# Dealing an expert's rows over the DMA engines from four starting points in turn instead of one

## The reference, cut to what matters

```
idx = top_k(where(expert_mask, choice, -inf), 8)       # 8 of 64 experts for each of 512 tokens
w = 2.5 * s[idx] / sum(s[idx])
for each expert e:                                     # w_exp_up[e]: 1024x512, w_exp_down[e]: 256x1024, float32
    y = (silu(gate) * up) @ w_exp_down[e],  (gate, up) = split(u[tokens of e] @ w_exp_up[e])
    acc[tokens of e] += y * w
out = x + acc + shared_expert(u)
```

```
56 54 80 82 64 63 80 56 85 67 67 66 83 64 43 61 57 49 63 58 77 69 57 78 53 61 68 58 51 58 77 68
62 58 79 62 58 62 49 48 86 82 66 53 51 47 47 64 66 52 59 45 64 48 77 56 63 76 73 71 70 66 75 88
```

## Time and profile before

| | us |
|---|---|
| median of 3 runs | 1267.52 |
| lowest, highest | 1266.24, 1271.38 |
| the profiled execution, its own time | 1268.87 |
| its span in the trace | 1267.0 |
| PE busy | 1168.9 (92%) |
| DVE busy | 918.3 (72%) |
| ACT busy | 724.0 (57%) |
| POOL busy | 238.0 (19%) |
| weights and other direct transfers (q1) | 250.88 MB, 56.0% of 16 engines' span |
| gathers and scatters (q0) | 33.87 MB, 11.6% |

### The profile page before, as it was taken

One profiled execution on the slowest core, in us unless ns is written; L12 is line 12 of the kernel. 1 busy time (PEld: TensorE's weight loads), 2 busy tenths in 40 slices (PEclk: granted clock), 3 DMA queues, 4 the chain that ended last, 5 costly groups with the idle time before them and its releaser, 6 DMA issues.

```text
span 1267.0 us, 17831 instructions
## 1 busy us (share of the span) xinstructions
PE 1168.9 (92%) x5911; PEld 883.1 (70%) x5911; DVE 918.3 (72%) x1343; ACT 724.0 (57%) x926; POOL 238.0 (19%) x146
## 2 busy tenths in 40 slices
PE   4999998999999899898999999999999999999993
PEld 3699987766677788565777666667666666666662
DVE  4576477544433693667999999889889888988882
ACT  7443333334333322425778777777777777777772
POOL 1000000000000000001343342333333332333331
PEclk9999998999999999899999999999999999999998
DMA  6312231212121323727999999999999999999992
GB/s 215 125 58 93 83 112 47 75 59 66 33 67 64 120 100 100 286 76 265 345 353 349 359 365 358 352 347 347 345 342 353 351 343 350 341 345 346 345 291 35
DMA packets 133357, 285.29 MB, mean 225 GB/s; under 512 B 11876, under 2 KB 34424, under 8 KB 133316
## 3 DMA queue, kind: packets, MB, share of 16 engines
q1 hardware_dynamic: 118580, 250.88, 56.0%
q0 software_dynamic: 14736, 33.87, 11.6%
HBM read 272.11 MB, written 29.38 MB: 238 GB/s over the span
## 4 chain that ended last, share of the span: by engine, by line
PE 46%; DMA 31%; DVE 9%; ACT 7%; issue 4%; SPq 1%; DVEq 0%; POOL 0%; POOLq 0%; ACTq 0%
PE bank L1370 36%; DMA arena<-in_w_exp_up_dram 16%; DMA arena<-in_w_exp_down_dram 12%; ACT split L521 5%; DVE split L1258 4%; PE bank L1538 2%; PE bank L1565 2%; DMA arena<-u_rows,arena 2%; PE bank L1449 1%; ACT arena L521 1%; PE bank L1682 1%; PE bank L1550 1%; PE bank L1701 1%; DMA arena<-in_x_dram 1%; DVE arena L944 0%
## 5 line engine op out<-in xcount | busy, mean ns | idle before, releaser
L1258 DVE TENSOR_TENSOR split<-arena,split 128x2048 fp32r<-128x2048 f32 x192 | 438.9, 2287 | 70.1 <-ACT split L521 68.8
L521 ACT ACTIVATE split<-arena 128x2048 fp32r<-128x2048 f32 x192 | 366.9, 1917 | 93.5 <-DMA arena<-in_w_exp_up_dram 76.0
L1370 PE MATMUL bank<-split,gatheredT 128*96 128x512 f32 x1536 | 374.2, 399 | 7.2 <-DVE gatheredT L1265 3.0
L1370 PEld LDWEIGHTS bank<-split,gatheredT 128*96 128x96 f32 x1536 | 244.6, 163 | 112.2 <-issue 5.8
L1370 PE MATMUL bank<-split,hidT 128*96 128x512 f32 x768 | 191.9, 398 | 1.5 <-ACT arena L521 1.5
L474 POOL DMA_INDIRECT arena<-u_rows,arena x64 | 128.4, 2007 | 251.7 <-DVE arena L1274 194.1
L1370 PEld LDWEIGHTS bank<-split,hidT 128*96 128x96 f32 x768 | 119.1, 162 | 47.0 <-issue 1.6
L482 POOL DMA_INDIRECT out_dram<-arena x64 | 101.7, 1589 | 257.7 <-ACT arena L521 180.1
L1370 PE MATMUL bank<-hT_high,front_split 128*128 128x512 f32 x448 | 143.9, 403 | 0.8 <-DVE hT_low L852 0.8
L521 ACT ACTIVATE arena<-bank 96x512 f32<-96x512 f32 (+4 forms) x217 | 107.7, 532 | 57.5 <-PE bank L1370 29.2
L1370 PEld LDWEIGHTS bank<-hT_high,front_split 128*128 128x128 f32 x448 | 81.4, 189 | 28.1 <-issue 11.5
(11 more groups left out here) (237 smaller groups left out, 1346.1 us busy)
## 6 DMA issues: line engine op xcount, KB each, us to landing
arena<-in_w_exp_up_dram SPq DMA_DIRECT2D x128, 1024.0 KB
arena<-in_w_exp_down_dram SPq DMA_DIRECT2D x64, 1024.0 KB
arena<-in_w_in_dram SPq DMA_DIRECT2D x14, 1024.0 KB, 5.5
arena<-in_w_in_dram SPq DMA_DIRECT2D x10, 768.0 KB, 4.5
arena<-in_w_branches_dram SPq DMA_DIRECT2D x4, 1024.0 KB, 5.0
arena<-in_w_out_dram SPq DMA_DIRECT2D x4, 1024.0 KB, 4.9
arena<-in_x_dram SPq DMA_DIRECT2D x4, 512.0 KB, 5.4
arena<-in_w_mem_kv_dram SPq DMA_DIRECT2D x2, 1024.0 KB, 5.2
```

Source lines behind the costliest of these rows:

```text
L521: return nc.scalar.activation(o, i, ACT.Copy, **kw)
L1258: v.tensor_tensor(both[:, 1], raw[q % RAW], both[:, 0].bitcast(F32), ALU.subtract).then_inc(low_done, 1)
L1370: ins = mm(bank, left[a], right[b], start=first and q == 0, stop=last and q == 2)
```

## The change

Before, the place in the list alone sets the DMA engine: place 0 is always on engine 0, and an expert with 70 tokens gives five rows to engines 0 to 5 and four to the others. After, there are four row assignments. Expert e uses number e % 4 (`n % TURN`), in which place p lies on engine (p + 4 * (e % 4)) % 16: the dealing begins at engine 0, 4, 8 or 12. The order of the tokens in their list, the number of rows, and what is computed for each token are the same.

The assignment leaves the stack of seven square constants (128 x 896 words become 128 x 768), and the four are a constant of their own, 128 partitions x 4 x 96 words (196,608 bytes), loaded by SP with one more transfer into the place of `out_norm`. DVE waits for three small transfers (48) in place of two (32).

```diff
-    spread = np.where(c < ROWS, c % SHARE * DMA_ENGINES + c // SHARE, c)
-    square = np.stack([r == c, r + c == P - 1, np.broadcast_to(c, (P, P)), r < c, np.ones((P, P)), level,
-                       np.broadcast_to(spread, (P, P))], 1)
+    square = np.stack([r == c, r + c == P - 1, np.broadcast_to(c, (P, P)), r < c, np.ones((P, P)), level], 1)
...
+    row, turn = np.arange(ROWS)[None, :], np.arange(TURN)[:, None]
+    spread = row % SHARE * DMA_ENGINES + (row // SHARE - turn * (DMA_ENGINES // TURN)) % DMA_ENGINES
...
+        "spread": np.ascontiguousarray(np.broadcast_to(spread, (P, TURN, ROWS)), dtype=np.float32),
...
-        square = at(take(7, P), 7, P)
-        ident, flip, counting, before, ones, level, spread = (square[:, n, :] for n in range(7))
+        square = at(take(6, P), 6, P)
+        ident, flip, counting, before, ones, level = (square[:, n, :] for n in range(6))
...
-        out_norm = at(take(BV), BV)
+        out_norm_at = take(BV)
+        out_norm = at(out_norm_at, BV)
+        spread = at(out_norm_at, TURN, ROWS)
...
             sp.dma_start(rs[:, 616:620], const["tokens"]).then_inc(c_in[9], 16)
+            sp.dma_start(spread, const["spread"]).then_inc(c_in[9], 16)
...
-            dve.wait_ge(c_in[9], 32)
+            dve.wait_ge(c_in[9], 48)
...
-                v.tensor_tensor(select[:, n % 2, :, :], bcast(spread[:, None, 0:ROWS], P, NT, ROWS),
+                v.tensor_tensor(select[:, n % 2, :, :], bcast(spread[:, n % TURN, None, :], P, NT, ROWS),
```

## The result

The changed kernel takes 1252.85 us (median of 4 runs, 1252.08 to 1253.92) against 1266.88 before (1265.52 to 1271.38): 14.0 us less, ratio 0.9884, 95% interval 0.9858 to 0.991. The direction was right, the size was not: 14.0 us in place of 8.8. Run again later it took 1252.04 beside 1266.95 (0.9884, 0.9863 to 0.9904), 14.9 us less.

A forecast was written before the change was run, and what follows sets the result against it. The prediction took the busiest DMA engine to bound the expert stage. Dealing gained 8.8 us, all other parts nothing: 1268.87 - 8.8 = 1260.1 us profiled, 1259 us as a median, range 1253.5 to 1266.5.

The forecast's parts named there:

- what bounds: Expert stage: goes at the DMA engines' pace, 10.4 us an expert against PE's 9.7 to 9.9; engine 0 fullest, 283 rows.
- the price of a row: Gathers and scatters on queue q0: 0.267 us a row in one direction, 0.53 us for gather and scatter.
- the sum's single term: Dealing from engine 0, 4, 8, 12: fullest engine 266 rows in place of 283, 8.8 us gained.
- A: Rival: DMA engines share one limit, so even dealing gives nothing; 1267.5 us, give or take 2; chance 0.12.
- The constants: Smaller square constant, 65,536 bytes less before the first weights: 0 to 0.3 us gained, taken as nothing.
- the limit that the prediction cites: Trainium skill page: memory side binds transfers at about 358 GB/s a core; if so, no gain, 1267.5 us.
- B: Rival: compute side, PE at 9.9 us an expert, takes half of the 8.8 us; 1263 us; chance 0.15.
- C: Rival: lag averages out, all DMA engines run at the mean, 14 us gained; 1253.5 us; chance 0.08.
- D: Rival: an engine slow by itself, such as 15, loses its cover; slower, 1275 us at a 23 us handicap; chance 0.03.
- the tail: Sign at the end of the weight stream: DMA share drops at once, without some five slices at 1 or 2 tenths.
- ACT's last waits: Sign at the end of the stream: ACT's waits of 1 to 2 us for the last weight blocks shrink.
- The time before 600 us: Sign for the part before 600 us: the same as before the change within 1 us.

The follow-up runs named there:

- filling up 15 engines beside the busiest: Changed kernel, empty rows of all engines gather row 511, against only engine 0's rows doing so: 1289.29 us against 1282.85.
- added gathers: Changed kernel (1252.04 us) with empty rows gathering row 511: 1282.85 us for engine 0's rows only, 1289.29 for all engines.
- added scatters: Changed kernel with scatters to a scratch table, 1255.20 us; the same with every empty row scattered too, 1286.81 us.
- only engine 0 filled: Changed kernel with only engine 0's empty rows gathering row 511: 1282.85 us, beside 1266.98 for the kernel before.

## Why the prediction came out wrong in size

**Right: what bounds.** The stage is bound by the DMA engines and, for most of the time, by the busiest. One, two and four starts are faster in the order of their fullest totals (sixteen against four is within the noise), the lags between the engines are those of the row totals, and filling up 15 engines beside the busiest costs only 6.4 us. The start at engine 8 shows that the fullest total is not all: the same total took 6 us more.

**Right: the price of a row.** 0.53 us in the forecast, 0.53 to 0.59 by the pairs of kernels with added gathers and with added scatters. With 0.32 and 0.27 the step of 17 gathers and 16 scatters is 9.8 us, with 0.26 and 0.27 it is 8.7.

**Wrong: the sum's single term.** The step that failed is "17 gathers and 16 scatters leave the path: 33 x 0.267 = 8.8 us". The dealing alone is 13.8 us, 4 to 5 more. By the trace the excess builds up between experts 20 and 50: at block 60 (expert 20) the fullest total is 6 rows lower than before, 3.2 us at the forecast's price, and 1.5 us are gained; at block 150 (expert 50) it is 15 rows, 8.0 us, and 12.2 are gained; at the end 14.2.

The rate shows the same. The two kernels are alike up to 800 us and 3% apart after it. The forecast had the earlier trace rows for this and used the fall from 360 to 344 only as evidence against A. The sum that lies in it was not made. From 800 to 1200 us the kernel before runs at a mean of 347; at the 360 of its best stretch the same bytes take 400 x 347 / 360 = 386 us, 14 us less, and its tail from 1200 to 1238 us, at 275, would take 9 us less. That is an upper end, 23 us. At the 357 that after reached in these 400 us it is some 11 us. Two sums for one thing, 8.8 by the busiest engine and up to 23 by the rate, should have stood side by side, with a forecast between them and a wider range.

**What carries the 4 to 5 us is open.** That the busy engine's own packets get slower when the others are far ahead (L) is not shown and not refuted. For it: weights at 45.5 us a MB with only engine 0 filled. Against it: that kernel was 9 us faster than L asked, though the 6.4 us that the others' rows cost may hide some of it, and two starts gain no more than their rows at the price. A fixed handicap of engine 8 would make the four starts gain less, not more. A dearer scattered row on the fullest engine is a third possibility that no run tried.

**The constants:** forecast 0 to 0.3 us, measured 1.2 and 2.7 us with intervals that reach from a loss of 1 to a gain of 4; part of the 14.0 may be theirs.

**The rivals.** A (one shared limit, no change) is refuted as the limit of the kernel before, which ran at 344 to 349 GB/s after 800 us and gained 14 us at the same bytes. The forecast's other ground was weak: 360 GB/s in one stretch does not contradict the limit that the prediction cites. After the change the rate holds at 358 to 361 for 300 us, so a shared limit of that size may well stand next behind the busiest engine. B is refuted too: the gain was not halved; PE went from 95 to 98% busy without taking the chain. C, all engines at the mean, had the right time, 1253.5, at a chance of 0.08. That is luck: its mechanism is not what happened. A tail of four slices is left, and the parts of a block still land up to 8.4 us apart, where C wanted the lags to average out. D did not decide. Its premise, that engines differ by themselves, holds in part: with sixteen starts the totals lie within 5 rows (2.7 us at the price), and the parts land up to 6.9 us apart.

**The signs forecast:** the tail shortened but did not vanish; ACT's last waits did not shrink; the late rate rose further than the 350 to 355 forecast, except in the last stretch (351); landing times in the chain stayed at 15 to 18 us; the added transfer hid. The time before 600 us was not the same within 1 us: block 12 was issued 3.8 us earlier. In the kernels with all starts at 0 and the new constants it was issued at 595.8 and 596.7 us, so this is not shown to be the constants' doing.

## What to carry to other kernels

Where transfers are split over 16 engines, the fullest engine's total over the whole stage sets most of the time, not the balance within one transfer: rotate the remainder. When a rate falls during a steady stage, work out what the stage would take at its best rate and set that beside the sum by parts. An average of packet times over all engines rises when their loads are uneven, and is no price of the busiest engine's packets. When two executions are laid side by side, take the difference from a mark at the start of the stage, not from the start of the program.

## What the runs showed of the hardware

The same dealing shifted by eight engines (283 rows on engine 8 in place of engine 0) took 1271.7 us in place of 1264.9 and 1265.8. With sixteen starts and totals within 5 rows, the 16 parts of a block landed 3.4 us apart in blocks 12 to 29 and 6.9 us apart in blocks 150 to 185. In the other profiled execution of that kernel, which took 1257.04 us where the median is 1248.80, one part landed 4.2 us after all the others. DMA engines of one core, given nearly the same work, do not keep step.

With uneven loads the light engines got at most 9 to 10 us ahead of the last one (before: 12 of 15 between 8.0 and 9.1 us; with only engine 0 filled: all 15 between 8.1 and 10.1), while the DMA share stayed at 1.03 to 1.04.

A load of 16 adjacent partitions with 4 KB each, twice for each expert on top of the stream, cost 64.6 us for 128 packets an engine, 0.5 us each, where 4 KB of a weight block record 0.16 to 0.17 us. Why was not tried.
